# Second prompt tile's PEER gathers by pair instead of by token, summed on VectorE and TensorE

## The reference, cut to what matters

```python
sc, j = lax.top_k(cand, P_TOPK)
eid = jnp.take_along_axis(cid, j, axis=-1)
g = jax.nn.softmax(sc.astype(F32), axis=-1)
act = jax.nn.gelu(jnp.einsum('td,thkd->thk', xc, u_tab[eid]).astype(F32))
return jnp.einsum('thk,thkd->td', g * act, v_tab[eid].astype(F32)).astype(h.dtype)
```

## Time and profile before

| | |
|---|---|
| runs | 2353.83, 2356.2, 2350.49 us (median 2353.83) |
| span of the profiled execution | 2353.7 us |
| TensorE, VectorE, ScalarE, GpSimd busy | 87%, 50%, 28%, 43% |
| HBM | 524.69 MB read, 2.69 MB written, 224 GB/s over the span |
| last hidden product ends, layer 0 and 1 | 721.4 and 1916.1 us |
| second half of X's last tile added, layer 0 and 1 | 1180.6 and 2350.5 us |

### The profile page before, as it was taken

The page is one execution under the profiler, slowest core; times in us unless marked ns, Lnnn a source line. Parts: engine busy times, 40 slices in busy tenths (PEclk is TensorE's granted clock), DMA queues, the critical chain, the costliest instruction groups (busy, mean ns, idle before and its releaser), DMA issues.

```text
span 2353.7 us, 38380 instructions
## 1 busy us (share of the span) xinstructions
PE 2044.5 (87%) x14289; PEld 1496.2 (64%) x14289; DVE 1177.2 (50%) x3447; ACT 650.0 (28%) x977; POOL 1001.2 (43%) x874
## 2 busy tenths in 40 slices
PE   9889999999997667889898889999999986777777
PEld 4554899999995323334356346999999973233332
DVE  2554699423333533578456834997233333333333
ACT  1332244545551001112134022454555520000000
POOL 0111469830004565656514303688500026666665
PEclk9899999999998798999997989999999998888878
DMA  6473434444447999999932334244444469999998
GB/s 233 173 279 119 144 129 159 161 162 162 168 163 264 331 355 369 362 329 335 350 122 62 90 116 152 81 161 153 162 168 164 165 217 348 360 346 357 365 357 312
DMA packets 179914, 529.91 MB, mean 225 GB/s; under 512 B 22066, under 2 KB 49234, under 8 KB 179474
## 3 DMA queue, kind: packets, MB, share of 16 engines
q0 software_dynamic: 87296, 310.68, 36.3%
q1 hardware_dynamic: 91282, 216.25, 26.8%
q10 hardware_dynamic: 1152, 0.52, 0.1%
HBM read 524.69 MB, written 2.69 MB: 224 GB/s over the span
## 4 chain that ended last, share of the span: by engine, by line
PE 68%; another core or an unknown queue 8%; DVE 8%; POOL 5%; issue 5%; DMA 3%; ACT 2%; SPq 1%; DVEq 0%; ACTq 0%; PEldq 0%
PE bank L950 10%; PE bank L952 10%; PE bank L951 10%; PE bank L769 8%; PE bank L1014 8%; PE bank L990 4%; POOL u_low L703 3%; PE bank L1032 3%; PE bank L1092 2%; DVE i_one_hot L2172 2%; DMA v_slot<-in_peer_v,v_rows 2%; POOL v_slot L712 2%; PE bank L979 1%; PE bank L1242 1%
## 5 line engine op out<-in xcount | busy, mean ns | idle before, releaser
L712 POOL DMA_INDIRECT v_slot<-in_peer_v,v_rows x417 | 394.6, 946 | 703.8 <-PE bank L952 441.1
L950 PE MATMUL bank<-h_parts,u_high 128*128 128x288 f32 x2048 | 607.0, 296 | 7.9 <-POOL u_low L703 6.2
L951 PE MATMUL bank<-h_parts,u_high 128*128 128x288 f32 x2048 | 604.4, 295 | 0.0
L952 PE MATMUL bank<-h_parts,u_low 128*128 128x288 f32 x2048 | 602.8, 294 | 0.0
L950 PEld LDWEIGHTS bank<-h_parts,u_high 128*128 128x128 f32 x2048 | 384.1, 188 | 11.6 <-POOL u_low L703 9.6
L952 PEld LDWEIGHTS bank<-h_parts,u_low 128*128 128x128 f32 x2048 | 385.8, 188 | 0.0
L951 PEld LDWEIGHTS bank<-h_parts,u_high 128*128 128x128 f32 x2048 | 384.6, 188 | 0.0
L1597 ACT CAST u_high<-u_slot 128x1024 fp32r<-128x1024 f32 x256 | 268.7, 1050 | 400.5 <-PE bank L952 249.1
L703 POOL TENSOR_TENSOR u_low<-u_slot,u_high 128x1024 fp32r<-128x1024 f32 x120 | 321.1, 2686 | 93.5 <-ACT u_high L1597 93.4
L1014 PE MATMUL bank<-v_slot,weight_columns 128*32 128x512 f32 x1412 | 274.1, 687 | 57.3 <-DMA v_slot<-in_peer_v,v_rows 34.1
L1014 PE MATMUL bank<-v_slot_of_columns,weight_columns 128*32 128x512 f32 x636 | 246.2, 687 | 69.8 <-DVE weight_columns L2179 44.0
(11 more groups left out here) (393 smaller groups left out, 2463.2 us busy)
## 6 DMA issues: line engine op xcount, KB each, us to landing
u_slot<-in_peer_ut SPq DMA_DIRECT2D x256, 512.0 KB, 3.5
w_q<-in_peer_w_q SPq DMA_DIRECT2D x8, 2048.0 KB, 14.4
region<-in_cache_a_kt SPq DMA_DIRECT2D x8, 960.0 KB, 11.8
region<-in_cache_a_v SPq DMA_DIRECT2D x8, 960.0 KB, 11.4
v_slot<-in_peer_v,v_rows POOLq DMA_INDIRECT x417
region<-in_ev_w_in SPq DMA_DIRECT2D x3, 2048.0 KB, 15.1
region<-in_pool_kv POOLq DMA_DIRECT2D x40, 128.0 KB, 5.0
ckv_t_norm<-in_pool_ckv SPq DMA_DIRECT2D x64, 64.0 KB
```

The lines of the kernel that those rows point to most:

```text
L712: pool.indirect_dma_start(out=VS[l][slot], out_offset=None, in_=v_rows, in_offset=bass.IndirectOffsetOnAxis(ap=IDX[:, at:at + 1], axis=0)) ...
L950: pe.matmul(bank, uh, HR[:, 0, c, :], start=(c == 0), stop=False)
L951: pe.matmul(bank, uh, HR[:, 1, c, :], start=False, stop=False)
L952: ins = pe.matmul(bank, ul, HR[:, 0, c, :], start=False, stop=(c == KC - 1))
```

## The change

In both layers tile 1 (tokens 128 to 255) is handled in another way. Its gathers, now the last 128 of each layer, fetch for pair k the rows of all 128 tokens, one token per partition. All weights of tile 1 are therefore made first: its 32 pick groups are put between the other groups (`PICKS`, from the seventh group on), their results collected in `picked_pairs`, turned once on TensorE and multiplied with the gates (`token_weights`). A gather is then summed by VectorE, which multiplies the slot with a column of weights and adds in PSUM (1024 wide), or, for every third k (layer 0) or fourth (layer 1) between 16 and 119, by TensorE with a diagonal matrix that ScalarE makes. Beside it: the one-hots are made by ScalarE in two passes for all groups, VectorE's picking writes into PSUM, one wide spread replaces four, values lag three picks, the clears are gone, `turn_route` makes a second bank per tile, each gather uses one of 8 semaphores in turn, and all key norms stand in the second part.

```diff
+MAIN = [(2, j) for j in range(NS // 4)] + [(0, j) for j in range(P // 4)]
+PICKS = []
+for m_, group_ in enumerate(MAIN):
+    PICKS.append(group_)
+    if 6 <= m_ < 38:
+        PICKS.append((1, m_ - 6))
...
+GATHERS = [(t_, 4 * j_ + i_) for t_, j_ in MAIN for i_ in range(4)] + [(1, k_) for k_ in range(P)]
+MAIN_GATHERS = 4 * NMAIN
+LANDINGS = 8
...
+def by_tensor(l, k):
+
+    return 16 <= k < P - 8 and k % (4 if l else 3) == 1
...
-        V_COLUMNS = ([(12.0, HB[0] + 8192, "s5_factors_made", 2, 34)]
-                     + [(16.3 + 8 * m, HB[0] + D * m, "picked_full", 16 + 8 * m, 37) for m in range(3)]
...
+        V_COLUMNS = ([(75.0, HB[0] + 8192, "s5_factors_made", 2, MAIN_GATHERS - 1)]
+                     + [column_slot(0, m, k, MAIN_GATHERS - 1) for m in (2, 3) for k in range(2)]
+                     + [column_slot(1, m, k, len(GATHERS)) for m, k in ((0, 1), (1, 1), (2, 1), (3, 1), (3, 0))],
+                     [column_slot(2, 0, k, len(GATHERS)) for k in range(4)]
+                     + [column_slot(0, m, k, len(GATHERS)) for m in range(4) for k in range(4)])
...
-                    sp.wait_ge(sem("v_used"), NGR - 1)
+                    sp.wait_ge(sem("v_used_by_dve"), USED_BY_DVE[0] - 6)
                     load(W_LATENT1, I["od_w_in"][:, :, 512:ODD_IN], "ident_then_w_in1_loaded")
                     load(W_IN1, I["od_w_in"][:, :, 0:512], "x_then_odd_loaded0")
...
+                for g, ((t, k), (slot, signal, count)) in enumerate(zip(GATHERS, V_PLAN[l])):
+                    name, landed = landing(l, g)
                     pool.wait_ge(sem(signal), before_layer[signal] + count)
-                    at = hidden_column(t)
+                    if landed > 16:
+
+                        pool.wait_ge(sem(name), landed - 16)
+                    at = P * t + k
...
                     ins.then_inc(d_full, 1)
+                    bank = to_dve()
+                    for i in range(4):
+                        out = bank[group_rows(t), i * P:i * P + P]
+                        if t < 2:
+                            ins = pe.matmul(out, ident[:, i:P:4], ROUTE[:, t, 0, :], start=True, stop=True)
+                        else:
+                            ins = pe.matmul(out, ident32[:, i:NS:4], I1B, start=True, stop=True)
+                    ins.then_inc(d_full, 1)
...
+                        pe.wait_ge(sem("diagonal_ready"), n)
+                        pe.wait_ge(sem(name), landed)
+                        for h in range(2):
+                            ins = pe.matmul(banks[6 + h][:, :], DIAG[:, n % 4, :], VS[l][V_PLAN[l][g][0]][:, 512 * h:512 * h + 512],
+                                            start=(TURN[l][k] == 1), stop=(TURN[l][k] == USED_BY_PE[l]), skip_group_check=True)
+                        ins.then_inc(sem("v_used_by_pe"), 1)
...
-                for k in (4, 6, 7):
-                    clear(banks[k])
-                for q in range(NGR + 2):
+                for q in range(NGR + 3):
                     if q < NGR:
                         spread_i1(q)
...
+                    for m in range(NMAIN):
+                        if PLACE[MAIN[m]] + 3 == q:
+                            values(m)
...
+                link(act.activation(flat, banks[q % 2][:, :], ACT.Abs, bias=NPCOL))
+                act.activation(flat, flat, ACT.Relu, bias=ONE, scale=-1.0).then_inc(sem("one_hot_ready"), 1)
...
+                        act.activation(DIAG[:, n % 4, :], ident, ACT.Copy, scale=WT[:, k:k + 1]).then_inc(sem("diagonal_ready"), 1)
...
+                            ins = dve.scalar_tensor_tensor(out=ACC_DVE[:, :], in0=slot, scalar=w, in1=ACC_DVE[:, :], op0=ALU.mult, op1=ALU.add)
+                        ins.then_inc(sem("v_used_by_dve"), 1)
...
+                    if j == P // 4 - 2:
+                        add_sums_of_tokens("v_used_by_pe", sum(USED_BY_PE[0:l + 1]), ACC_PE)
+                        say("pe_sums_added")
```

445 lines of the change are left out of this document (264 added, 181 removed).

## The result

The changed kernel took 2386.76 us (median of four runs, 2382.82 to 2391.44), the kernel before 2352.16 beside it: a ratio of 1.0166, 95% interval 1.0141 to 1.0191. It is slower by some 35 us; 2354 was predicted, with a range of 2331 to 2372. The profiled execution has a span of 2381.6 us, 27.9 more than that of before.

A forecast was written before the change was run, and what follows sets the result against it. Gather stages were taken as DMA-bound (356 GB/s in layer 1), hidden stages as TensorE-bound; terms -5 + 5 - 4 - 1 + 6 - 1 = 0 on a 2353.7 us span gave 2354 us, range 2331 to 2372.

The forecast's parts named there:

- the first part: Samples and tile 0, 160 gathers per layer: TensorE's 4.9 us fits a four-gather group's 5.9 us, so cost 0.
- rival (4): First part of the gather stages: TensorE becomes the bound at a lower clock, +45 or +18 us (2372 us); chance 0.10.
- rival (3): Layer 0's second part: VectorE becomes the bound, deciding above 1.6 us a sum; at 1.9 us, 2388 us; chance 0.07.
- Layer 1's -1: Layer 1's second part (tile 1, 128 gathers): sums on VectorE and TensorE fit beside the gathers, gaining 1 us.
- rival (2): Tile 1's new gathers move faster, at 410 GB/s: 2318 us, with half the gain 2336 us; chance 0.12.
- Layer 0's -4: Layer 0's second part (tile 1, 128 gathers): 4 of the 11 us lost there come back, range -11 to +5.
- End of layer 0: From layer 0's last gathers to the add: +2 for VectorE's last work, +6 in all with queue sharing (+2 to +10).
- My sum of 8.9 us: End of layer 0: VectorE's last sum, two reciprocals (3.5), turned tiles (2.9) and a wide add (1.25).
- The +4 for two queues: End of layer 0: weight loads share the DMA engines with the gathers, which land 4 us later at two thirds rate.
- the start in layer 0: Start of the gather stage: first values earlier with clears dropped and one-hots on ScalarE, -2.5 us a layer.
- the routing: Inside the hidden stage: extra TensorE products and waits for banks, +2.5 us a layer, +5 in all (+3 to +9).
- The end of layer 1: After layer 1's last gather: one sum and one add follow the landing, -1 us (-2 to +1).

The follow-up runs named there:

- the level without them: Changed kernel (its added empty instructions left no trace) against the kernel before with pair rows, kernel before at 2264.45 us: 2288.16 us, 1.0086.
- that group: Runs beside a kernel before of 2355.04 us: changed kernel again 2392.70 us (1.0151); with slot dates at the measured pace 2372.92 us (1.0071).
- the 2264 us group: Four runs beside a kernel before of 2264.45 us, gathers at 409 GB/s: one-hots on VectorE 1.0171, more ScalarE code 1.0086, pair rows 1.0009, later s5 slot 1.0053.

## Why the prediction was wrong

*The step that failed* is the first part, "Cost 0, hidden by the DMA queue as long as TensorE runs at 2.4 GHz". It measured +12.2 and +12.4 us. I had added up TensorE's instructions (4.9 of 5.9 us fits) and taken the sum for the pace. But a group now needs two rounds of spread, one-hot, pick and VectorE's picking, with a signal between each, in an order fixed on every engine, where it needed one. Leaving out the second tile's rounds in layer 1 brought back 224.6 us; leaving out three quarters of their products did not. So rival (4), TensorE as the bound because of its clock, had the place right and the mechanism wrong: the clock granted there, 0.89 and 0.88, is above the 0.85 and 0.86 of the earlier trace rows. That it is the waiting for signals within a round that costs the time is argued from the order of waits, not shown by itself: the long gaps go with the rounds too. They are not all of it, since at the level without them layer 1's first part was still 8.2 us longer. In layer 0 the rounds were not left out; there the slot dates are shown to cost about 10 us (below). The one-hot is also dearer than priced, 0.69 and 0.72 instead of 2 x 0.60; that adds to the round, but moving it to VectorE changed nothing in sum.

*Slots.* "Layer 0 keeps nine to twelve slots for most of this part, as before" was true of their number and missed their dates. The table expects a group of picks each 5.2 us; they came each 6.3 in layer 1 (237.1 us for 151 gathers), so gathers were queued behind slots not yet free: 10.1 us for the s5 slot, 11.7 and 14.0 us for picks. Moving the dates gave back 20 of the 38 us lost in that group, 18 of them in layer 0's two parts. The diff showed such a date (75.0), and the earlier trace rows the real pace.

*Second part.* The VectorE sum took 1.29 us (1.27 predicted), and rival (3) never came near its 1.6. Layer 1's -1 was -10.9: rival (2) in its effect, but the rows fetched are not the cause. What I took for a property of the gathers, 356 GB/s at full share, depends on what runs beside them: products added on TensorE in the changed kernel's second part brought 408 to 411 GB/s down to 351 to 377 in all but one of the stretches at a full DMA share. It isn't TensorE's busy time in general, though: the direct loads at 410 in the earlier trace rows ran beside a TensorE busy 9.79 of 10 us, and in the 2264 us group the gain was -1.1 us, since the kernel before's gathers had 409 GB/s there. Layer 0's -4 was +1.5: GpSimd waits there 21.8 us for diagonal products (L1092) and 13.9 for VectorE's sums (L2316), where it waited 19.5 for values before. Giving 17 of the sums to TensorE took 10 us off the part, so VectorE's sums are part of it.

*End of layer 0*, +6 predicted, +9.0 measured, but for another reason than the turns between queues. VectorE's rows at the end:

```profile
1181.66 0.69 DVE L1966 TENSOR_SCALAR key_scale<-banks 128x512 f32<-128x512 f32 x1 [2.33 <-remote]
1182.56 5.26 DVE L2316 SCALAR_TENSOR_TENSOR banks<-v_slot,token_weights,banks 128x1024 f32<-128x1024 f32 x4 [0.21 <-DVE key_scale L1966]
1187.73 1.21 DVE L1963 TENSOR_TENSOR keep<-keep,banks 128x1024 f32<-128x1024 f32 x1
...
1190.10 1.64 DVE L1966 TENSOR_SCALAR odd_tokens<-keep 32x1024 f32<-32x1024 f32 x2
1191.96 1.29 DVE L2316 SCALAR_TENSOR_TENSOR banks<-v_slot,token_weights,banks 128x1024 f32<-128x1024 f32 x1 [0.22 <-DVE odd_tokens L1966]
1193.29 1.29 DVE L2316 SCALAR_TENSOR_TENSOR banks<-v_slot_of_columns,token_weights,banks 128x1024 f32<-128x1024 f32 x1
1194.61 2.62 DVE L2316 SCALAR_TENSOR_TENSOR banks<-v_slot,token_weights,banks 128x1024 f32<-128x1024 f32 x2
1197.13 3.54 DVE L2146 RECIPROCAL key_scale<-key_scale 128x256 f32<-128x256 f32 x2
...
1203.63 1.22 DVE L1963 TENSOR_TENSOR keep<-keep,banks 128x1024 f32<-128x1024 f32 x1 [0.24 <-DVE odd_turned L1963]
```

and TensorE's first product of the next block, behind them:

```profile
1203.79 5.89 PE L1343 MATMUL banks<-w_latent,odd_turned 128*128 128x416 f32 x10 [9.87 <-DVEq L1960]
```

VectorE is without a pause of more than 0.3 us from 1182.6 to 1204.9. It is late with its sums, not waiting for the gathers: by the trace's DMA packets the last gather had landed at 1188.4, and the last four sums begin at 1191.96. My sum of 8.9 us began with the last of them; the wide add and the odd tile's scaling ahead of them, 4.2 us from 1187.73, were not in it. The +4 for two queues sharing the DMA engines did not happen: the first packet of the weight loads is at 1187.2, 1.2 us before the gathers' last, and that one came 4.9 us after the last gather's issue at 1183.5, where it had been 6.1 us before the change. So the term came near for the wrong reason.

*What held*: the start in layer 0 (-2.3 for -2.5), the routing (+3.4 for +5). In layer 1 the start gained nothing (-0.1): the tenth gather still waits 4.3 us for the first values. The end of layer 1 was +2.8 for -1; the add of TensorE's half stands there ahead of the last four sums and begins 2.1 us after VectorE is free, though by its records TensorE's last product had ended 7.5 us before it.

Of the 27.9 us: 24.6 from the first parts, -9.4 from the second parts, +11.8 from the two ends, -2.4 from the starts, +3.4 from routing, and -0.1 from the rest.

## What to carry to other kernels

An engine with a quarter of its time free can still hold up a pipeline when each of its steps waits for an answer from another engine. Count rounds of signals per item, not only instructions, and test by leaving out a whole round as well as its work: here the two gave different answers. Where a table of expected times decides which buffer a transfer waits for, a change of pace anywhere makes it wrong, so its dates belong to the change. A transfer rate read in one setting need not be the rate the transfer has when the work beside it changes.
